# Token squares on ScalarE, later parameter blocks, and RWKV keys transposed by VectorE with a block exchange through DRAM, in a four-layer hybrid backbone

## The reference

```python
def rmsnorm(x, g, eps=NORM_EPS):
    xf = xf * lax.rsqrt(jnp.mean(xf * xf, axis=-1, keepdims=True) + eps)   # xf is x in float32
    return (xf * g).astype(x.dtype)

def rwkv7_scan(r, w, k, v, kk, a, s0):      # 16 heads of 64, two directions
    def step(s, inp):
        r_t, w_t, k_t, v_t, kk_t, a_t = inp
        s_kk = jnp.einsum('bhvk,bhk->bhv', s, kk_t)
        s = (s * w_t[:, :, None, :] - s_kk[..., None] * (kk_t * a_t)[:, :, None, :]
             + v_t[..., None] * k_t[:, :, None, :])
        return s, jnp.einsum('bhvk,bhk->bhv', s, r_t)

for i in range(DEPTH):                       # kind = i % 3; adaLN: silu(c) @ ada_w[i] + ada_b[i]
    hl = modulate(xl, norm1_g[i], ml[0], ml[1])      # ml, mc: the six adaLN rows
    yc, yl = mixer(hc, hl)                           # rwkv7, ssd, window attention, rwkv7
    xl = xl + ml[2] * yl
    xl = xl + ml[5] * conv_ffn(modulate(xl, norm2_g[i], ml[3], ml[4]), ...)
```

## Time and profile before

| | us |
|---|---|
| median of three runs | 3620.71 (3611.99 to 3623.83) |
| the profiled execution | 3625.17 |
| its span from first to last instruction | 3623.4 |
| TensorE busy | 3453.8 (95%) |
| VectorE busy | 2500.4 (69%) |
| ScalarE busy | 1154.7 (32%) |
| GpSimd busy | 596.4 (16%) |

### The profile page before, as it was taken

The page is one execution under the profiler, slowest core; times in us unless marked ns, Lnnn a source line. Parts: engine busy times, 40 slices in busy tenths (PEclk is TensorE's granted clock), DMA queues, the critical chain, the costliest instruction groups (busy, mean ns, idle before and its releaser), DMA issues. The chain is left out here.

```text
span 3623.4 us, 74330 instructions
## 1 busy us (share of the span) xinstructions
PE 3453.8 (95%) x28645; PEld 2520.7 (70%) x28645; DVE 2500.4 (69%) x4570; ACT 1154.7 (32%) x2478; POOL 596.4 (16%) x1135
## 2 busy tenths in 40 slices
PE   7998998999999999999999999999999997888999
PEld 2447777588886455555888866678877546777887
DVE  7986665489897657563898955469986956664431
ACT  3034664223302444431233014323310235663210
POOL 2015553000000323320000000000000105552000
PEclk9998999999999999999999999999999999999999
DMA  6641111244453323223434520044434531111454
GB/s 204 210 144 21 23 24 32 71 128 126 126 163 96 100 83 102 79 78 99 128 124 127 163 81 27 27 125 130 126 119 127 180 118 25 24 24 27 133 152 134
DMA packets 584315, 365.07 MB, mean 101 GB/s; under 512 B 126144, under 2 KB 553480, under 8 KB 581928
## 3 DMA queue, kind: packets, MB, share of 16 engines
q1 hardware_dynamic: 557544, 250.40, 25.0%
q0 software_dynamic: 26432, 110.07, 8.7%
HBM read 348.73 MB, written 11.67 MB: 99 GB/s over the span
## 5 line engine op out<-in xcount | busy, mean ns | idle before, releaser
L274 PE MATMUL PS<-H,WR 128*128 128x512 f32 (+1 forms) x1424 | 477.1, 494 | 0.0
L567 DVE SCALAR_TENSOR_TENSOR WORK<-WORK,SC 128x512 f32<-128x512 f32 x616 | 418.4, 746 | 0.7
L274 PEld LDWEIGHTS PS<-H,WR 128*128 128x128 f32 x1424 | 267.9, 190 | 187.5 <-issue 167.2
L2525 PE MATMUL PS<-WORK 64*64 64x64 f32 (+2 forms) x6944 | 365.4, 233 | 27.6 <-ACT BIG L2822 17.3
L547 POOL DMA_DIRECT2D WORK<-in_ada_w_dram x88 | 66.2, 752 | 1831.0 <-DVE WORK L567 1013.9
L1450 PE MATMUL PS<-BIG,WR 128*128 128x512 f32 (+1 forms) x944 | 329.4, 503 | 4.8 <-DVE BIG L1074 1.5
L2525 PEld LDWEIGHTS PS<-WORK 64*64 64x64 f32 (+1 forms) x6944 | 286.2, 141 | 66.8 <-ACT WORK L2811 23.0
L1450 PEld LDWEIGHTS PS<-BIG,WR 128*128 128x128 f32 x944 | 175.7, 190 | 132.2 <-issue 112.0
L2811 ACT ACTIVATE WORK<-PS 128x64 f32<-128x64 f32 (+3 forms) x528 | 161.5, 325 | 300.4 <-PE PS L2525 295.6
L988 ACT ACTIVATE WORK<-PS 128x512 f32<-128x512 f32 x252 | 135.1, 541 | 346.7 <-PE PS L921 314.4
L921 PE MATMUL PS<-BIG 128*128 128x256 f32 x984 | 223.9, 380 | 0.0
(11 more groups left out here) (362 smaller groups left out, 6420.6 us busy)
## 6 DMA issues: line engine op xcount, KB each, us to landing
WORK<-in_ada_w_dram POOLq DMA_DIRECT2D x88, 1024.0 KB, 6.2
WR<-in_ffn_w_in_dram SPq DMA_DIRECT2D x220, 256.0 KB, 2.9
BIG<-in_ffn_w_in_dram SPq DMA_DIRECT2D x132, 256.0 KB, 3.4
WR<-in_ffn_w_out_dram SPq DMA_DIRECT2D x106, 256.0 KB, 2.8
WR<-in_ssd_w_in_dram SPq DMA_DIRECT2D x96, 256.0 KB, 2.8
BIG<-scratch_dram POOLq DMA_DIRECT2D x8, 2048.0 KB, 8.0
BIG<-in_ffn_w_out_dram SPq DMA_DIRECT2D x36, 256.0 KB, 3.1
BIG<-in_ada_w_dram SPq DMA_DIRECT2D x4, 2048.0 KB, 18.8
```

The lines of the kernel that those rows point to most:

```text
L274: mm = pe.matmul(outs, WR[:, slot, k, 0:m], rhs(k), start=first and k == 0, stop=last and k == nk - 1)
L567: lag(vec.scalar_tensor_tensor(ACC3[:, s_], w, by, ACC3[:, s_], ALU.mult, ALU.add), label)
L2525: return pe.matmul(o, lhs, rhs, start=start, stop=stop)
```

## The change

It has two parts.

**At the start**, ScalarE squares the inputs as they were loaded, with tokens on partitions, and sums each token's squares in the same instruction (four instructions of 128x1024). Four small ones put these sums on diagonals of an identity, in the place from which TensorE takes the mean. GpSimd's seven additions and ScalarE's eight squares of transposed blocks are gone. VectorE sums four input blocks of eight, TensorE multiplies four. The parameter blocks are split: the first four (14 DMAs) are loaded ahead of the fourth quarter, and the other twelve are transposed and copied behind the last row.

**In both RWKV layers** `by_token` leaves TensorE, and its copies leave ScalarE. VectorE transposes the 32x32 blocks of the keys instead (step TB, `vec.transpose`, 128x256 each, four in each slot), at k = 6, 8, 10 and 12 of the first slot and k = 0, 1, 3 and 9 of the second. This puts the two off-diagonal blocks of each head's 64x64 matrix in the wrong place, and SP exchanges them through DRAM: four stores of 64 KB (`swap_out`) and, when they have landed, four loads (`swap_in`). `chain_s` waits for the loads, and reads each chunk's keys with a step of four elements.

```diff
+            params(PARAM_ORDER[:4], first_loaded, "params0")
+            load(3)
...
+            def token_squares(c):
+                act_last()
+                s(act.activation(WORK[:, 13824:14848], XIN[:, c, :], ACT.Square, accum_out=MSQ[:, c:c + 1]))
...
-                early += [... (9, "H2", both[0], 0),
-                          (12, "HB", both[0], 0, 0), (15, "HB", both[0], 0, 1), (16, "H2", both[1], 0),
-                          (18, "HB", both[1], 0, 0), (20, "HB", both[1], 0, 1)]
+                late += [(k, "TB", i, 0, d, n) for k, (d, n) in zip((6, 8, 10, 12), ((0, 1), (1, 1), (0, 0), (1, 0)))]
...
+            def swap_out(i, s_):
+                sp.wait_ge(vec_done, C.at(f"{t}.t{i}.tb{s_}"))
+                if i:
+                    sp.wait_ge(swap_loaded, C.at(f"{t}.t{i - 1}.bk{s_}"))
+                for b in range(4):
+                    sp.dma_start(swap[s_, b ^ 1], BK[32 * b:32 * b + 32, s_, :, :, 1 - b % 2, :]).then_inc(
+                        swap_stored, C.mark(swap_stored, f"{t}.t{i}.swap{s_}" if b == 3 else None, 16))
+            def swap_in(i, s_):
+                sp.wait_ge(swap_stored, C.at(f"{t}.t{i}.swap{s_}"))
+                for b in range(4):
+                    sp.dma_start(BK[32 * b:32 * b + 32, s_, :, :, 1 - b % 2, :], swap[s_, b]).then_inc(
+                        swap_loaded, C.mark(swap_loaded, f"{t}.t{i}.bk{s_}" if b == 3 else None, 16))
             for i in range(KD):
                 grams_out(i, 0)
                 blocks_in(i, 0)
                 if i == 0:
                     grams_out(i, 1)
                     blocks_in(i, 1)
+                else:
+                    swap_out(i - 1, 1)
+                    swap_in(i - 1, 1)
                 inverse_out(i, 0)
                 inverse_in(i, 0)
                 if i:
                     grams_out(i, 1)
                     blocks_in(i, 1)
+                swap_out(i, 0)
+                swap_in(i, 0)
                 inverse_out(i, 1)
                 inverse_in(i, 1)
+            swap_out(KD - 1, 1)
+            swap_in(KD - 1, 1)
...
+            def by_token(i, s_, d, n):
+                half, q = SEGS[s_], 2 * i + d
+                vec_last()
+                if i:
+                    vec.wait_ge(pe_done, C.at(f"{t}.{q - 2}.sp{min(4 * s_ + 3, NQ - 2)}"))
+                src = (SD if n else ADS[i % 2])[:, d, half].rearrange("p (c b t) -> p b c t", b=2, t=32)
+                dst = BK[:, s_, d, n].rearrange("p a (f c) -> p a c f", c=4)
+                lag(vec.transpose(dst, src), f"{t}.{q}.turned{s_}" if n else f"{t}.t{i}.tb{s_}" if d else None)
```

More of the change, by code:

```diff
@@ L351, in start_sp, with params @@
                 in_loaded, C.mark(in_loaded, "inputs", 16))
-            for q in range(1, 4):
-                load(q)
+            def params(order, loaded, label):
+                for b in order:
+                    r = 0
+                    for n, part in enumerate(blocks[b]):
+                        sp.dma_start(ST[r:r + part.shape[0], b, :], part).then_inc(
+                            loaded, C.mark(loaded, label if (b, n) == (order[-1], len(blocks[b]) - 1) else None, 16))
+                        r += part.shape[0]
+            load(1)
+            load(2)
+            params(PARAM_ORDER[:4], first_loaded, "params0")
+            load(3)
             sp.dma_start(K[:, 2 * P:], a["consts"][:, 2 * P:]).then_inc(
                 vec_loaded, C.mark(vec_loaded, None, 16))
[L356 to L361, removed]
+            params(PARAM_ORDER[4:], vec_loaded, "params")
         def start_pe():
@@ L406, in start_pe @@
             pe.wait_ge(in_loaded, C.at("inputs"))
-            for k in range(KD):
+            for k in range(3):
                 transposed(k)
@@ L410, in start_pe @@
             by_input(1)
+            for k in range(3, KD):
+                transposed(k)
+            norm_pe("n10", "ada", 0)
             by_sum(1)
-            norm_pe("n10", "ada", 0)
             by_input(2)
@@ L423, in start_pe @@
             leave((pe_done, w_used), "ada")
+            pe.wait_ge(vec_loaded, C.at("params"))
+            for n in range(1, 4):
+                params(n)
         def start_pool():
-            for k in range(1, KD):
-                pool.wait_ge(act_done, C.at(f"xs{k}"))
-                g(pool.tensor_tensor(SS, XSQS[0] if k == 1 else SS, XSQS[k], ALU.add), "ada.ss" if k == KD - 1 else None)
             leave((pool_done,), "ada")
@@ L448, in start_act, with params @@
             row(2)
-            for n in range(4):
+            def params(n):
                 act.wait_ge(pe_done, C.at(f"pt{n}"))
@@ L454, in start_act @@
                       f"par{4 * n + j}")
+            params(0)
             row(3)
             leave((act_done,), "ada")
+            for n in range(1, 4):
+                params(n)
         def over_inputs(acc, src, label, i, n=KD):
@@ L2946, in rwkv_act @@
                         stage_first(staging, u)
-            run({**staging, "GT": grams, "HB": by_token, "Z": z_step, "W": chain_w, "S": chain_s, "YE": y_end,
+            run({**staging, "GT": grams, "Z": z_step, "W": chain_w, "S": chain_s, "YE": y_end,
                  "P1": post1, "P2": post2, "P2e": post2e})
```

79 lines of the change are left out of this document (35 added, 44 removed).

## The result

| | before | after |
|---|---|---|
| median, us | 3620.59 (3611.99 to 3623.83) | 3738.43 (3734.04 to 3744.40) |
| the profiled execution, us | 3625.17 | 3734.04 |
| mean granted clock of TensorE | 0.985 | 0.970 |

A forecast was written before the change was run, and what follows sets the result against it. First slots were taken as bound by the chain through SP that brings the inverses, second slots by TensorE and the recurrence. Pairs at +25 us and the start at -7 gave +18, forecast 3638 us, range 3600 to 3662.

The forecast's parts named there:

- start: Squares and sums before the first modulated block: work removed there saves 7 us, bounds 0 and -12.
- `by_token` leaves TensorE: RWKV slots: 59 us of TensorE work gone, worth a net 1.35 us in each second slot, hidden in first slots.
- transpositions on VectorE, packed: Four VectorE transpositions of about 0.4 us in each slot, partly in idle time: 0.5 us charged to each second slot.
- case of its own: TensorE's strided key loads in `chain_s`: nothing in the sum; rival slower still, 3663 us with 25 us added, chance 0.13.
- all that lengthens the first slots: Exchange in SP's queue delays half 1's inverses: first slots grow by 4.7 us in layer 0, 4.1 in layer 3.
- the length of the exchange: Four stores, then four loads on SP: 3.4 us plus 2.0 us, together 5.4 us.
- the upper bound of 6.6: Longest exchange on SP in us, from 0.59 us for each issue and 2.2 us to land.
- A baseline of one slot: First slot lengths before the change, read from one pair in each layer: 20.2 us in layer 0, 20.6 in layer 3.
- the worth of the second slots: Second slots, taken as bound by TensorE and the recurrence, shrink by 1.35 us to 23.7 (layer 0) and 21.6 (layer 3).
- the lateness of E: VectorE's step E of half 1, waiting for loaded inverses: 24.9 us behind half 0's E, 24.7 in layer 3.
- Pair 7: RWKV pair without staging: its exchange starts early enough and its second slot gains 1.35 us in both layers, -2.7 us.
- The limit of the second exchange: Half 1's exchange, in second slots, must end before the next pair's inverses: 21.3 us to the next E, no cost yet.

The follow-up runs named there:

- e1: Kernel before with only the start's part of the change: 3615.7 us, ratio 0.9989.
- e8: Kernel before with `by_token` and its copies left out, nothing in their place, step S multiplying zeros: 3630.1 us, ratio 1.0027.
- e3: Changed kernel without the exchange, turned keys written and read packed instead of with a step of four, values left out: 3625.6 us, ratio 1.0016.
- e2: Changed kernel without the exchange, keys still with the step of four, zeros multiplied instead of values and removals: 3649.6 us, ratio 1.0090.
- e10: Changed kernel with earlier transpositions, packed keys and 48 useless TensorE products in each second slot: 3617.1 us, ratio 1.0003.
- e11: Changed kernel with the exchange issued by ScalarE instead of SP, at the same transpositions: 3782.4 us, ratio 1.0468.
- e12: Kernel before without `by_token`, with 8 useless products at each of the eight places where its parts stood: 3615.0 us, ratio 0.9992.
- e7: Changed kernel with earlier transpositions, packed keys and 24 useless TensorE products in each second slot: 3628.3 us, ratio 1.0018.

## Why the prediction was wrong

The sign was right, and so was the place of the wait; the size was off by a factor of six and a half. The parts, from the runs:

| part | forecast, us | measured, us | from |
|---|---|---|---|
| start | -7 | -4 | e1 |
| `by_token` leaves TensorE | in the pairs' sum, -1.35 a second slot | +10 | e8 |
| transpositions on VectorE, packed | in the same 1.35 | 0 | e3 less e1 and e8 |
| step of four, reading and writing | 0 (case of its own) | +24 | e2 less e3 |
| exchange | all that lengthens the first slots | +89 | after less e2 |
| together | +18 | +119, directly +118 | |

The parts are differences of one chain of runs, so their sum has to come out at the whole; it confirms nothing. A part is its cost in this order, and the 0 of the transpositions is a balance: beside e8, e3's second slots in layer 0 are 1.4 us longer and its first slots 0.5 us shorter.

By slots, over pairs 1 to 6 of both layers, 28 us were forecast and 95.5 us came. The first slots are 2.7 and 2.2 us longer than forecast (27.6 for 24.9, 26.9 for 24.7), 29 us in all. The second slots are 3.2 and 3.3 us longer (26.9 for 23.7, 24.9 for 21.6), 39 us in all: the larger miss.

- **The step that failed first: the length of the exchange.** The place was right, and so was the mechanism: SP holds the inverses back until the last load is issued. But four DMAs take 2.5 us and more to issue, 0.6 to 0.9 us each, not the 0.5 us taken from the store of the same size. In pair 4 of layer 0 the loads begin 500.50 - 496.21 = 4.3 us behind the first store (3.4 taken), and take 2.9 us themselves (2.0 taken): 7.2 us. The means are 7.0 and 7.7 us, above the upper bound of 6.6. In layer 0 the start was 0.9 us late and the way from the store to E 0.2 us longer; in layer 3 both were as forecast.
- **A baseline of one slot.** 20.2 and 20.6 us were first slots of one pair each; over pairs 1 to 6 they are 21.3 and 21.0. So the 4.7 and 4.1 us named for their growth do not fit the sum, which sets 48.6 and 46.3 us against the mean pairs: in it the first slots grow by 3.6 and 3.7 us, and the runs showed 6.3 and 5.8.
- **The step that failed second, and cost more: the worth of the second slots.** They were to shrink by 1.35 us, and grew by 1.5 and 2.3 us. "Bound by TensorE and the recurrence" was taken to mean that each microsecond taken from TensorE comes back. e8 shows that none does: removing `by_token` lengthened layer 0's second slots by 0.9 us and layer 3's by 0.3. The account asked what TensorE's freed time is worth on the path, and not what it does to the clock.
- **What the lateness of E triggers.** The prediction stopped at E. It did not say that TensorE would stand idle for 7 us and run its next work at 1.2 GHz. No run parts this price from that of the wait, but the traces bound it. The low clock lies in the second slots, and these came out 1.0 us shorter in layer 0 and 1.1 us longer in layer 3 than in e2; 80 of the 89 us are in the first slots, which run at 1.00 and 0.98. So most of the 89 us is the wait. In e2 pair 4's first and second slot read:

```profile
464.04:485.61 21.57, 20.09 (x455) 16.81 (x451) 17.27 (x41) 13.30 (x31) 13.45 (x32) 1.00 0.08 12
485.61:514.08 28.47, 23.58 (x524) 20.54 (x522) 19.55 (x44) 12.15 (x34) 10.47 (x31) 0.94 0.16 29
```

- **Pair 7.** Its exchange was to start early enough. Its first slots took 23.0 and 24.3 us, against 19.9 and 22.0 before and 16.8 and 18.3 in e2: it was held up like the others.
- **The step of four at nothing.** The reason given, that a column already takes two cycles, did not hold; the bound of 55 ns for each load was about right (65 measured). The case for it was priced at 25 us with a chance of 0.13. That its price agrees with the 24 us measured is partly luck, since these hold VectorE's writing too, which the case left out; it belonged in the sum.
- **The limit of the second exchange**, 21.3 us, stood just under the 21.6 us forecast for layer 3's second slots, and hardly showed: E of half 0 waits for the inverses by 2 us at most in the rows of pairs 1 and 7 above, since those slots are long for other reasons.
- **The start** was right in the trace (6.7 us of 7), and its 4 us at the end are at the limit of what e1 can tell.

No version beats the kernel before by more than its measurement can tell: of those that compute the whole, e1, at 0.9989, is the nearest, and the change with early transpositions, packed keys and filler (e10) is level with it at 1.0003.

## What to carry to other kernels

Before work is taken off a nearly full engine, look at what it would do with the time: if the next thing that it waits for comes no sooner, the time becomes idle, and TensorE's granted clock can fall with it and take back what the work had cost, as in e8. A transfer that is put into an in-order queue costs by what stands behind it, not by its bytes: place it where its data are ready long before the next urgent one, and do not move its wait to an engine that carries the recurrence. When the sum holds a row's duration for a new pattern, such as four DMAs in succession or a read with a step, take the mean over many slots for the baseline, and expect a piece in a series to take longer than a lone one: even the upper bound made of lone rows was too low here.

## What the runs showed of the hardware

- Loads of 64x64 float32 weights with 16 bytes from element to element took 207 ns (e2) against 142 ns packed (e3); VectorE's 32x32 transposition of 128x256 took 646 ns when it wrote with that step, 446 ns packed.
- Four DMAs of 64 KB in succession took 2.5 to 3.6 us to issue on SP (after) and 2.5 to 3.7 us on ScalarE (e11), although lone ones of that size took 0.36, 0.47 and 0.59 us on SP before.
- TensorE's granted clock fell to 0.5 in the last part of a wait of 7.2 us (after), and also at the end of one of 2.4 us (e8); with filler around a wait of 1.75 us it stayed at 1.00 (e12). Useless 64x64 products at such places made a kernel 12 (e7) and 17 us (e10) faster.
